# Compression tiles alternated with projection tiles, a start in halves, and the gated output moved ahead of two remainders

## The chip, the cores and the metric

One NeuronCore of a Trainium2 chip runs the whole program; seven stay idle. The metric is the device time of one execution in microseconds (us), the median of several runs. The profile is of one further execution. TensorE does matmuls, VectorE is called DVE, ScalarE ACT, GpSimd POOL and SyncE SP.

## What is computed

Two transformer blocks over 256 tokens of width 2048, all in fp32. The change touches the first block only, and of it these parts:

```python
def compress(kraw, pe, w1, w2):
    kb = kraw[:, idx] + pe[None, None, :, None, :]
    hdn = jax.nn.silu(jnp.einsum("bnlhd,ldf->bnhf", kb, w1))
    return jnp.einsum("bnhf,fe->bnhe", hdn, w2)

h = rmsnorm(x, norm_w[layer])
proj = h @ w_in[layer]
(u_pool, g_pool, q, kc_raw, vc_raw, k_sel, v_sel, k_win, v_win,
 g_nsa, g_br) = jnp.split(proj, split_at, axis=-1)
kc = rope(compress(heads(kc_raw, N_KV_HEADS), ...), cmp_pos)
vc = compress(heads(vc_raw, N_KV_HEADS), ...)
o_nsa = nsa_attention(qh, kc, vc, ksh, ..., kwh, ..., gates)
y_b = (o_nsa * jax.nn.silu(g_nsa)) @ w_nsa_out[layer]
```

`nsa_attention` has three branches (compressed keys, selected keys, window) over 16 query heads in 4 groups. Beside the blocks a modulation is computed, `mod = silu(c) @ w_ada + b_ada`, which the second block needs; its weights are multiplied on DVE.

## The kernel before

**Weight tiles.** All weights that TensorE multiplies lie in one array `ws` of 128 x 1024 tiles (512 KB), in the order of use. SP loads them into a ring of four (`raw`). ACT writes the high part `w_hi` of each (`split`, line 619), DVE the remainder `w_lo` (`split`, line 1065), and TensorE multiplies `w_hi` with `a_hi`, `w_lo` with `a_hi` and `w_hi` with `a_lo` (`tile`, lines 1805 to 1807): 12 matmuls of 512 columns for a projection tile. Semaphores bind the ring: a load waits for `lo_done` of the tile four before, ACT for the load and for `tile_used` of the tile four before, DVE for `hi_done`, TensorE for `lo_done`. `steps` on ACT and DVE writes the splits of the next tiles; what stands between two calls of it is done between two tiles. `PHASES` gives the order of the tiles, `CHUNKS` the numbers of the PSUM pairs (two pairs in turn; a pair is free when it has been evicted, semaphore `acc_free`).

**The start.** The activations are read as `x0` in four chunks. TensorE transposes them in eight turns (`x_turn`, line 1844 in the trace), ACT scales them into `a_hi` (line 832) and DVE makes `a_lo` (line 1273). Turn j + 2 stands behind tile j. The identity and the norm weights `n1T` come by POOL's queue (line 456); TensorE, ACT and DVE wait for both (`first_in`).

**Compression.** After the projections `kc`, `vc`, `ks`, `kw`, `vs`, the eight tiles `cmp_k` multiply the blocks of the compressed keys (`kb_hi`, `kb_lo`, 60 rows): 12 matmuls of 256 columns each. `vw` follows, then the eight of `cmp_v`, then the tile `gbr` (branch gates) and `q` in four chunks. The blocks are built on DVE (`block_sum`, `block_lo`) and ACT (`kb_hi`), in one buffer for both, so those of the values follow the use of the first.

**Attention.** A loop over the four groups. In each, three chunks of weight tiles (24) fill the places between four units of attention. `a.fill` gives the tiles at each place. Unit j's probabilities are transposed and multiplied in step j + 1; after it come the gated output `ot` (DVE, line 1246), `y_hi` (ACT, line 806) and `y_lo` (DVE, line 1250). The third step and the last lie at j = 3 and j = 4. Chunks 1 and 2 are merge gates: DVE adds `bias_c` to the PSUM halves into `gst` (lines 1135 and 1138), which frees each half for the next chunk (`half_free`, `half2_free`); the next group's first tile waits for them. Six halves of modulation weights (`ada`, ring of three) are multiplied and summed on DVE in each group (`modulation`, line 1079).

**POOL's queue** issues in order, in each turn of its loop (`nsa_loads`): six loads of `ada`, each waiting until the modulation that read its slot of the ring is done, then twice a load of the next `bias_c` (256 KB, line 502), each after a `gate_sum`:

```python
for k in range(loads):
    load_ada(at_i(ADA0["nsa"] + ADA_RING + k))
for c in range(2):
    pool.wait_ge(gate_sum, 2 * i + c + 1)
    pool.dma_start(bias_c[:], ...).then_inc(bias_c_in, 16)
```

The sixth `load_ada` waits for `ada_used` of this group's sixth modulation. The last group has only three loads ahead of its two of `bias_c`.

## Time and profile before

| | |
|---|---|
| median of 3 runs | 2280.42 us (2279.46 to 2280.89) |
| profiled execution | 2282.75 us, span 2281.1 us |
| TensorE (PE) busy | 2250.8 us, 99% |
| DVE busy | 1556.1 us, 68% |
| ACT busy | 1105.4 us, 48% |
| bytes moved | 546.49 MB, mean 240 GB/s |
| chain that ended last | PE 87%, DVE 6%, ACT 3%, issue 2%, DMA 2% |

The span runs from the first to the last instruction; the time of the execution has 1.65 us more around it. Matmuls overlap in the records: a 512-column one lasts 0.39 us and the next starts 0.23 us after it, so a wait shows in full only where it is longer than that overlap. In a timeline the bracket gives the engine's idle time ahead of a row and what ended it.

### The profile page before, as it was taken

The page shows a single profiled execution, that of the slowest core. Times are in us where ns is not written, and L with a number is a line of the kernel's source. Part 1 is how long each engine was busy: PE and PEld are TensorE (multiplying, and loading weights), DVE is VectorE, ACT ScalarE, POOL GpSimd, SP SyncE. Part 2 cuts the span into 40 slices and gives each one's busy share as a digit, 9 for nine tenths or more (in the row PEclk, how much of TensorE's full clock was granted, in tenths as well). Part 3 has the DMA queues.
Part 4 walks back from the last instruction along what each step waited for, and adds up shares of the span by engine and source line. Part 5 has one row for each costly group of instructions (what it writes and reads, how often), then busy time and mean ns, then how long its engine had stood idle before and what let it go on. Part 6 is the DMA issues. An engine that isn't in the chain of part 4 may idle for free.

```text
span 2281.1 us, 31278 instructions
## 1 busy us (share of the span) xinstructions
PE 2250.8 (99%) x10377; PEld 1863.9 (82%) x10377; DVE 1556.1 (68%) x1936; ACT 1105.4 (48%) x1437; POOL 149.9 (7%) x285
## 2 busy tenths in 40 slices
PE   8999999999999999999999999999999999999998
PEld 6888888788788888888888888888888888888886
DVE  5685777777776556788777776666555666655566
ACT  6454445566564444533366554445444443444444
POOL 1000110000000000011011210000000000000000
PEclk9999999999999999999999999999999999999999
DMA  8887897555665766598588886666666666666564
GB/s 286 288 283 266 302 337 253 205 193 202 211 225 175 272 209 228 199 320 292 195 284 288 311 317 248 235 217 213 210 212 221 230 222 228 227 213 208 207 205 146
DMA packets 150104, 546.49 MB, mean 240 GB/s; under 512 B 17249, under 2 KB 17392, under 8 KB 148496
## 3 DMA queue, kind: packets, MB, share of 16 engines
q1 hardware_dynamic: 112400, 406.37, 51.4%
q0 software_dynamic: 34752, 129.71, 16.3%
q10 hardware_dynamic: 2880, 9.44, 1.0%
q8 instruction: 46, 0.75, 0.1%
q14 instruction: 26, 0.21, 0.0%
HBM read 534.92 MB, written 10.53 MB: 239 GB/s over the span
## 4 chain that ended last, share of the span: by engine, by line
PE 87%; DVE 6%; ACT 3%; issue 2%; DMA 2%; DVEq 0%; ACTq 0%; SPq 0%
PE ps L1805 22%; PE ps L1807 22%; PE ps L1806 22%; PE ps L1922 5%; PE ps L1924 5%; PE ps L1923 5%; DVE w_lo L1065 2%; PE ps L1844 2%; DMA raw<-ws_dram 2%; ACT prob L787 1%; ACT w_hi L619 1%; PE ps L1981 1%; PE ps L2028 1%; DVE prob L1226 1%; PE ps L1822 0%
## 5 line engine op out<-in xcount | busy, mean ns | idle before, releaser
L1065 DVE TENSOR_TENSOR w_lo<-raw,w_hi 128x1024 fp32r<-128x1024 f32 x761 | 927.8, 1224 | 617.5 <-ACT w_hi L619 599.7
L619 ACT ACTIVATE w_hi<-raw 128x1024 fp32r<-128x1024 f32 x753 | 795.7, 1061 | 996.5 <-PE ps L1807 859.8
L1805 PE MATMUL ps<-w_hi,a_hi 128*128 128x512 f32 x1632 | 638.6, 391 | 3.4 <-DVE w_lo L1065 1.7
L1807 PE MATMUL ps<-w_hi,a_lo 128*128 128x512 f32 x1632 | 636.2, 390 | 0.0
L1806 PE MATMUL ps<-w_lo,a_hi 128*128 128x512 f32 x1632 | 636.0, 390 | 0.0
L1805 PEld LDWEIGHTS ps<-w_hi,a_hi 128*128 128x128 f32 x1632 | 306.9, 188 | 67.1 <-issue 2.2
L1807 PEld LDWEIGHTS ps<-w_hi,a_lo 128*128 128x128 f32 x1632 | 306.9, 188 | 64.1
L1806 PEld LDWEIGHTS ps<-w_lo,a_hi 128*128 128x128 f32 x1632 | 307.1, 188 | 63.1
L1922 PE MATMUL ps<-w_hi,a_hi 128*128 128x512 f32 x640 | 258.5, 404 | 0.4 <-DVE w_lo L1065 0.4
L1924 PE MATMUL ps<-w_hi,a_lo 128*128 128x512 f32 x640 | 249.8, 390 | 0.0
L1923 PE MATMUL ps<-w_lo,a_hi 128*128 128x512 f32 x640 | 249.3, 390 | 0.0
L1924 PEld LDWEIGHTS ps<-w_hi,a_lo 128*128 128x128 f32 x640 | 120.1, 188 | 25.9
L1922 PEld LDWEIGHTS ps<-w_hi,a_hi 128*128 128x128 f32 x640 | 120.3, 188 | 24.8 <-issue 1.1
L1923 PEld LDWEIGHTS ps<-w_lo,a_hi 128*128 128x128 f32 x640 | 120.4, 188 | 24.3 <-issue 1.0
L1079 DVE CUSTOM_DVE_ANT_0 ada<-ada,cb 128x1024 f32<-128x1024 f32 x108 | 131.8, 1220 | 6.4 <-DVE nms L1200 3.7
L1805 PE MATMUL ps<-w_hi,f_hi 128*128 128x512 f32 x336 | 130.8, 389 | 0.0
L1807 PE MATMUL ps<-w_hi,f_lo 128*128 128x512 f32 x336 | 130.7, 389 | 0.0
L1806 PE MATMUL ps<-w_lo,f_hi 128*128 128x512 f32 x336 | 130.7, 389 | 0.0
L1086 DVE CUSTOM_DVE_ANT_0 ada<-ada,cb 128x1024 f32<-128x1024 f32 x84 | 102.5, 1221 | 25.1 <-DMA ada<-wa_dram 24.3
L472 POOL DMA_DIRECT2D ada<-wa_dram x105 | 55.7, 531 | 715.5 <-DVE mod_part L1079 643.6
L1807 PEld LDWEIGHTS ps<-w_hi,f_lo 128*128 128x128 f32 x336 | 63.1, 188 | 13.2
L1806 PEld LDWEIGHTS ps<-w_lo,f_hi 128*128 128x128 f32 x336 | 63.1, 188 | 13.1
(310 smaller groups left out, 2125.4 us busy)
## 6 DMA issues: line engine op xcount, KB each, us to landing
raw<-ws_dram SPq DMA_DIRECT2D x769, 512.0 KB, 4.2
ada<-wa_dram POOLq DMA_DIRECT2D x192, 512.0 KB, 4.8
gates_spill<-gst ACTq DMA_DIRECT2D x16, 512.0 KB, 5.4
ga<-gates_spill POOLq DMA_DIRECT2D x8, 512.0 KB, 4.2
gb<-gates_spill POOLq DMA_DIRECT2D x8, 512.0 KB, 6.0
bias_c<-b_merge_dram POOLq DMA_DIRECT2D x9, 256.0 KB, 4.9
x<-x_dram SPq DMA_DIRECT2D x4, 512.0 KB, 7.6
cb<-c_dram POOLq DMA_DIRECT2D x2, 1024.0 KB, 5.1
```

What stands on the lines that cost most here:

```text
L472: pool.dma_start(ada[:, k.slot(ADA_RING), :], wa[k.n]).then_inc(ada_landed[k.slot(ADA_RING)], 16)
L619: act.activation(w_hi[:, k.slot(RING), :], raw[:, k.slot(RING), :], ACT.Copy).then_inc(hi_done, 1)
L1065: dve.tensor_tensor(w_lo[:, k.slot(RING), :], raw[:, k.slot(RING), :], w_hi[:, k.slot(RING), :].bitcast(F32), ALU.subtract).then_inc(lo_do ...
L1079: dve.tensor_tensor_reduce(out=a, in0=a, in1=cb[:, half * TW:(half + 1) * TW], scale=1.0, scalar=0.0, op0=ALU.mult, op1=ALU.add, accum_out ...
L1086: dve.tensor_tensor_reduce(out=a, in0=a, in1=c[:, half * TW:(half + 1) * TW], scale=1.0, scalar=0.0, op0=ALU.mult, op1=ALU.add, accum_out= ...
L1805: pe.matmul(o, hi(m, tb), w_hi[:, s, cols], start=m == 0, stop=False)
L1806: pe.matmul(o, hi(m, tb), w_lo[:, s, cols], start=False, stop=False)
L1807: mm = pe.matmul(o, lo(m, tb), w_hi[:, s, cols], start=False, stop=m == of * kts - 1)
L1844: ins = pe.transpose(ps[0:m, bank, n * P:n * P + b.shape[0]], b, ident[0:b.shape[0], 0:b.shape[0]])
L1922: pe.matmul(o, hi, w_hi[:, s, cols], start=m == 0, stop=False)
L1923: pe.matmul(o, hi, w_lo[:, s, cols], start=False, stop=False)
L1924: mm = pe.matmul(o, lo, w_hi[:, s, cols], start=False, stop=m == KT - 1)
```

## The change

1. **Start.** `ident` and `n1T` become one tensor `first`, loaded first on SP's queue. The first chunk of `x` comes in two halves on ACT's queue, the first weight tile in two halves on SP's; after them SP's order is raw 1, x 1, raw 2, x 2, raw 3, x 3. ACT loads its table with a small copy ahead of the data. TensorE multiplies zeros (`idle_turns`): 11 products of 128 columns, then the first turn, then 7 more. The first tile is split and multiplied in halves, with the second turn between them.
2. **Compression.** `BESIDE` is the order of 16 tiles: two `cmp` tiles, then by turns a projection tile and a `cmp` tile, and two projection tiles at the end. `cmp_k` goes with `vw`, `cmp_v` with `q1`; `gbr` and `q0` come between the two. The loads of `ws` are laid out in that order. `kb_hi` and `kb_lo` of the values, the transposes of the hidden rows and the first modulations of `qup` move along.
3. **Attention.** In step j = 3, `ot` is computed ahead of the two remainders and no longer behind them, and the sixth modulation moves from ahead of them to behind `y_lo`.

```diff
+BESIDE = [(1, 0), (1, 1)] + [t for j in range(6) for t in ((0, j), (1, j + 2))] + [(0, 6), (0, 7)]
 PHASES = [
-    ("kcvc", 2 * T_K), ("ks", T_K), ("kw", T_K), ("vs", T_K), ("cmp_k", 8), ("vw", T_K), ("cmp_v", 8), ("gbr", 1),
-    ("q01", 2 * T_K), ("qup", 6 * T_K), ("nsa", 4 * 3 * T_K),
+    ("kcvc", 2 * T_K), ("ks", T_K), ("kw", T_K), ("vs", T_K), ("cmp_k_vw", 2 * T_K), ("gbr", 1),
+    ("q0", T_K), ("cmp_v_q1", 2 * T_K), ("qup", 6 * T_K), ("nsa", 4 * 3 * T_K),
...
-            for k in range(RING):
+            sp.dma_start(first[:], t["first"]).then_inc(first_in, 16)
+            sp.dma_start(raw[:, 0, 0:NC], ws[0][:, 0:NC]).then_inc(raw0_in, 16)
+            sp.dma_start(raw[:, 0, NC:TW], ws[0][:, NC:TW]).then_inc(raw_landed[0], 16)
+            for k in range(1, RING):
+                sp.dma_start(raw[:, k, :], ws[k]).then_inc(raw_landed[k], 16)
                 sp.dma_start(x0[:, k], x_chunks[k]).then_inc(x_in[k], 16)
-                sp.dma_start(raw[:, k, :], ws[k]).then_inc(raw_landed[k], 16)
...
+            act.dma_start(x0[:, 0, :, 0:S], x_first[:, :, 0:S]).then_inc(x0_in, 16)
+            act.dma_start(x0[:, 0, :, S:NC], x_first[:, :, S:NC]).then_inc(x_in[0], 16)
+            act.wait_ge(t_free, 2)
+            act.activation(warm[:], cmx[:], ACT.Copy)
...
             project("vs", 4)
             hidden(0)
+            evict(5, At(G0["vw"]), ACT.Copy)
             act.wait_ge(kb_sum, 2)
-            act.wait_ge(tile_used, T0["cmp_k"] + 8)
+            act.wait_ge(tile_used, T0["cmp_k_vw"] + 2 * T_K)
             act.activation(kb_hi[:], kbf[:], ACT.Copy).then_inc(kb_hi_done, 1)
...
-                        if nsa_ and j % 2:
-                            m = 3 * (j // 2) + 2
-                            modulation(ada0 + m, m)
+                        if nsa_ and j == 1:
+                            modulation(ada0 + 2, 2)
...
                     if nsa_:
+                        if j == nu - 1:
+                            gated(u0 + (j - 1), *a.units[j - 1])
                         fill(a.fill[2 + j])
...
+                            if j != nu - 1:
+                                gated(u, tb, h0)
+                            o = ot[:].rearrange("p (h s) -> p h s", h=2)
                         dve.wait_ge(a.y_hi_done, (u + 1 + 1).n)
                         dve.tensor_tensor(lo, o, hi.bitcast(F32), ALU.subtract).then_inc(a.y_done, 1)
+                    if nsa_ and j == nu - 1:
+                        modulation(ada0 + 5, 5)
...
+            pe.wait_ge(zeros_in, 1)
+
+            def idle_turns(n):
+                for _ in range(n):
+                    pe.matmul(ps[:, 7, 0:P], squares[:, 1, 0:P], squares[:, 1, 0:P], start=True, stop=True)
+
+            idle_turns(11)
+            pe.wait_ge(first_in, 16)
...
             x_turn(0)
-            x_turn(1)
-            for j in range(T_K):
+            idle_turns(7)
+            pe.wait_ge(t_free, TG["norm1"] + 3)
+            for q in range(2):
+                if q:
+                    pe.wait_ge(lo_done, 1)
+                else:
+                    pe.wait_ge(half0_lo, 1)
...
+                if q == 0:
+                    x_turn(1)
+            mm.then_inc(tile_used, 1)
+            x_turn(2)
+            for j in range(1, T_K):
...
+                for k, (of_kb, j) in enumerate(BESIDE):
+                    if of_kb:
+                        tile(At(T0[phase] + k), pair(At(g)), j, 8, lambda m, tb: kb_hi[:, m, :],
+                             lambda m, tb: kb_lo[:, m, :], kts=4, rows=CMP_ROWS, blocks=1, width=CMP_H)
+                    else:
+                        if j == 0:
+                            pe.wait_ge(acc_free, g + 2)
+                        tile(At(T0[phase] + k), pair(At(g + 1)), j, T_K, ah, al)
```

**How it moves the instructions.** TensorE from the program's first matmul on, before (x8 means eight in a row):

```order
L1844 MATMUL ps<-ident,x_137 128x128 x8
L1805 MATMUL ps<-w_hi,a_hi 128x512
L1806 MATMUL ps<-w_lo,a_hi 128x512
L1807 MATMUL ps<-w_hi,a_lo 128x512
```

and now (`squares` holds the zeros, `first` the identity):

```order
L2074 MATMUL ps<-squares 128x128 x11
L1878 MATMUL ps<-first,x_136 128x128 x4
L2074 MATMUL ps<-squares 128x128 x7
L2100 MATMUL ps<-w_hi,a_hi 128x512
L2101 MATMUL ps<-w_lo,a_hi 128x512
L2102 MATMUL ps<-w_hi,a_lo 128x512
L2100 MATMUL ps<-w_hi,a_hi 128x512
L2101 MATMUL ps<-w_lo,a_hi 128x512
L2102 MATMUL ps<-w_hi,a_lo 128x512
L1878 MATMUL ps<-first,x_136 128x128 x4
```

The eight transposes of `x` have become four and four, with products of zeros ahead of the first four and behind them, and the second four stand in the middle of the first tile.

DVE in compression, from the first `block_sum` of the values on, before:

```order
L1299 TENSOR_TENSOR kbf<-ckT,peT 128x15x16 x4
L1065 TENSOR_TENSOR w_lo<-raw,w_hi 128x1024 x4
L1299 TENSOR_TENSOR kbf<-ckT,peT 128x15x16 x4
L1065 TENSOR_TENSOR w_lo<-raw,w_hi 128x1024 x6
L1307 TENSOR_TENSOR kb_lo<-kbf,kb_hi 128x1920
L1065 TENSOR_TENSOR w_lo<-raw,w_hi 128x1024
```

and now:

```order
L1332 TENSOR_TENSOR kbf<-ckT,peT 128x15x16 x4
L1081 TENSOR_TENSOR w_lo<-raw,w_hi 128x1024 x6
L1332 TENSOR_TENSOR kbf<-ckT,peT 128x15x16 x4
L1081 TENSOR_TENSOR w_lo<-raw,w_hi 128x1024
L1095 ISA ada,mod_part<-ada,cb 128x1024
```

with this at the end of the phase and after it:

```order
L1081 TENSOR_TENSOR w_lo<-raw,w_hi 128x1024 x3
L1108 COPY mod_66<-mod_part 128x6
L1081 TENSOR_TENSOR w_lo<-raw,w_hi 128x1024 x3
L1340 TENSOR_TENSOR kb_lo<-kbf,kb_hi 128x1920
L1081 TENSOR_TENSOR w_lo<-raw,w_hi 128x1024
```

The second `block_sum` (`kbf`) stands two splits later, and `kb_lo` has moved from behind six more splits to behind the whole phase, `gbr` and two tiles of `q0`; three of the modulations (`ada`) now lie between the splits of the phase.

DVE at the end of a group, from the probabilities of the last unit to the merge gate of the last chunk, before:

```order
L1226 TENSOR_TENSOR prob<-prob,coef 128x1024
L1079 ISA ada,mod_part<-ada,cb 128x1024
L1079 ISA mod_part 128x1
L1065 TENSOR_TENSOR w_lo<-raw,w_hi 128x1024
L1065 TENSOR_TENSOR w_lo<-raw,w_hi 128x1024
L1246 TENSOR_TENSOR ot<-ps,gT 128x256
L1250 TENSOR_TENSOR y_lo<-ot,y_hi 128x2x128
L1065 TENSOR_TENSOR w_lo<-raw,w_hi 128x1024
L1065 TENSOR_TENSOR w_lo<-raw,w_hi 128x1024
L1135 SCALAR_TENSOR_TENSOR gst_160<-ps,rstd,bias_c 128x512
L1138 SCALAR_TENSOR_TENSOR gst_160<-ps,rstd,bias_c 128x512
```

and now:

```order
L1242 TENSOR_TENSOR prob<-prob,coef 128x1024
L1250 TENSOR_TENSOR ot<-ps,gT 128x256
L1081 TENSOR_TENSOR w_lo<-raw,w_hi 128x1024
L1081 TENSOR_TENSOR w_lo<-raw,w_hi 128x1024
L1272 TENSOR_TENSOR y_lo<-ot,y_hi 128x2x128
L1095 ISA ada,mod_part<-ada,cb 128x1024
L1095 ISA mod_part 128x1
L1081 TENSOR_TENSOR w_lo<-raw,w_hi 128x1024
L1081 TENSOR_TENSOR w_lo<-raw,w_hi 128x1024
L1151 SCALAR_TENSOR_TENSOR gst_159<-ps,rstd,bias_c 128x512
L1154 SCALAR_TENSOR_TENSOR gst_159<-ps,rstd,bias_c 128x512
```

`ot` moved up past the modulation and two remainders; the modulation's two rows moved down past these remainders and `y_lo`. POOL's loop, whose last `ada` load waits for that modulation, ends as before:

```order
L475 DMA ada<-wa_dram 128x1024
L475 ISA
L475 DMA ada<-wa_dram 128x1024
L504 ISA
L505 ISA
L505 DMA bias_c<-b_merge_dram 128x512
L504 REGISTER_ALU
L505 ISA
```

These rows are the last loads of the turn and then those of `bias_c`; nothing in their order has changed.

## Rows read from the trace of the kernel before

**Rows 1.** Page, part 1; part 5: line engine op, tiles xcount | busy, mean ns | idle

```profile
PE 2250.8 (99%) x10377; PEld 1863.9 (82%) x10377; DVE 1556.1 (68%) x1936; ACT 1105.4 (48%) x1437; POOL 149.9 (7%) x285
...
L1065 DVE TENSOR_TENSOR w_lo<-raw,w_hi 128x1024 fp32r<-128x1024 f32 x761 | 927.8, 1224 | 617.5 <-ACT w_hi L619 599.7
L619 ACT ACTIVATE w_hi<-raw 128x1024 fp32r<-128x1024 f32 x753 | 795.7, 1061 | 996.5 <-PE ps L1807 859.8
```

**Rows 2.** What TensorE waited for, whole span: total us, times, longest us

```profile
PE ps L1844 <- ACT pcT L640: 4.8, 4, 1.2
PE ps L1805 <- DVE w_lo L1065: 3.2, 3, 1.7
```

**Rows 3.** Timeline of the start: start us, us, engine, line, op [idle before <-releaser]

```profile
8.05 1.97 PE L1844 MATMUL ps<-ident,x 128*128 128x128 f32 x8 [8.05 <-DMA n1T<-n1T_dram]
9.42 0.82 ACT L832 ACTIVATE a_hi<-ps,n1T 128x256 fp32r<-128x256 f32 x2
10.76 0.87 DVE L1273 SCALAR_TENSOR_TENSOR a_lo<-ps,n1T,a_hi 128x256 fp32r<-128x256 f32 x2
11.69 0.80 PE L1805 MATMUL ps<-w_hi,a_hi 128*128 128x512 f32 x1 [1.67 <-DVE a_lo L1273]
...
16.97 0.62 PE L1844 MATMUL ps<-ident,x 128*128 128x128 f32 x4
17.35 0.48 PE L1805 MATMUL ps<-w_hi,a_hi 128*128 128x512 f32 x1
...
20.19 0.60 PE L1844 MATMUL ps<-ident,x 128*128 128x128 f32 x4
```

**Rows 4.** Loads of x at the start (to landing), and fp32 matmuls in a timeline

```profile
DMA to landing us min/median/max: 4.9/7.6/9.6
...
1288.90 1.95 PE L2022 MATMUL ps<-pt,proj 128*128 128x128 f32 x16
```

**Rows 5.** Timeline of the compression tiles, TensorE, and an eviction by ScalarE

```profile
127.72 0.28 PE L1805 MATMUL ps<-w_hi,kb_hi 128*60 128x256 f32 x1
127.84 0.28 PE L1806 MATMUL ps<-w_lo,kb_hi 128*60 128x256 f32 x1
...
130.41 0.68 ACT L845 ACTIVATE proj<-ps,rstd 128x512 f32<-128x512 f32 x1
...
141.97 0.47 PE L1805 MATMUL ps<-w_hi,a_hi 128*128 128x512 f32 x1 [1.73 <-DVE w_lo L1065]
...
175.00 0.33 PE L1805 MATMUL ps<-w_hi,kb_hi 128*60 128x256 f32 x1 [0.77 <-DVE w_lo L1065]
```

**Rows 6.** Last unit of group 0: DVE, GpSimd, bias loads (439.20; another alone), TensorE

```profile
436.63 1.23 DVE L1079 CUSTOM_DVE_ANT_0 ada<-ada,cb 128x1024 f32<-128x1024 f32 x1 [0.19 <-DVE prob L1226]
437.78 2.36 DVE L1065 TENSOR_TENSOR w_lo<-raw,w_hi 128x1024 fp32r<-128x1024 f32 x2
440.06 0.42 DVE L1246 TENSOR_TENSOR ot<-ps,gT 128x256 f32<-128x256 f32 x1
...
438.52 0.53 POOL L472 DMA_DIRECT2D ada<-wa_dram  x1 [4.28 <-DVE mod_part L1079]
439.20 0.54 POOL L502 DMA_DIRECT2D bias_c<-b_merge_dram  x1
...
bias_c<-b_merge_dram POOLq DMA_DIRECT2D x1, 256.0 KB, 5.2
...
bias_c<-b_merge_dram POOLq DMA_DIRECT2D x1, 256.0 KB, 4.1
...
444.85 0.75 DVE L1135 SCALAR_TENSOR_TENSOR gst<-ps,rstd,bias_c 128x512 f32<-128x512 f32 x1
...
447.53 0.58 PE L1922 MATMUL ps<-w_hi,a_hi 128*128 128x512 f32 x1
...
459.93 1.23 DVE L1065 TENSOR_TENSOR w_lo<-raw,w_hi 128x1024 fp32r<-128x1024 f32 x1 [0.84 <-ACT w_hi L619]
```

**Rows 7.** A weight load issued between 122 and 123 us: us to landing

```profile
raw<-ws_dram SPq DMA_DIRECT2D x1, 512.0 KB, 8.2
```

More of the change, by code:

```diff
@@ L178, in const @@
             return r
-        ident = const("ident", [P, P])
+        first = const("first", [P, P + KT])
+        ident, n1T = first[:, 0:P], first[:, P:P + KT]
         trig1 = const("trig1", [P, 2, TB, HALF])
@@ L187, in build @@
         cvalid = const("cvalid", [P, TB, N_CMP])
-        n1T = const("n1T", [P, KT])
         n1T_2 = const("n1T_2", [P, KT])
@@ L454, in _ @@
         def _(pool):
-            for dst, name in ((ident, "ident"), (n1T, "n1T")):
-                pool.dma_start(dst[:], t[name]).then_inc(first_in, 16)
             for c in range(4):
@@ L857, in hidden @@
                 act.sem_inc(hdn_ready, 1)
+                steps(k + (2 * T_K - 2), 2)
             def hidden_turned(n):
@@ L892, in _ @@
                 act.activation(gates[:, tb], ps[:, 7, tb * 3 * NQ:(tb + 1) * 3 * NQ], ACT.Sigmoid, scale=rstd[:, tb:tb + 1])
-            project("q01", 7, 1)
+            hidden(1)
+            evict(7, At(G0["q1"]), ACT.Copy)
+            project("qup", 8, 0)
+            hidden_turned(1)
+            project("qup", 9, 1)
             act.wait_ge(cmp_done, 2)
             act.activation(vc[:], ps[0:N_CMP, 5, :], ACT.Copy).then_inc(cmp_ready, 1)
-            with act.Fori(0, 2) as i:
-                for c in range(2):
-                    steps(At(T0["qup"] + c * T_K, 2 * T_K, i), T_K)
-                    evict(2 * i + (8 + c), At(G0["qup"] + c, 2, i), ACT.Copy)
+            for c in range(2, 4):
+                project("qup", 8 + c, c)
             for c in range(2):
@@ L1264, in _ @@
             link(dve.memset(vcg[:], 0.0))
+            dve.memset(squares[:, 1, 0:P], 0.0).then_inc(zeros_in, 1)
             dve.memset(nmax[:, :], 0.0).then_inc(acc_free, 3)
             dve.memset(cmx[:, :], 0.0).then_inc(t_free, 2)
-            dve.wait_ge(first_in, 32)
+            dve.wait_ge(first_in, 16)
             for r in range(8):
-                split(At(r))
+                if r:
+                    split(At(r))
                 dve.wait_ge(t_hi, TH["norm1"] + r + 1)
@@ L1276, in _ @@
                 lo.then_inc(t_free, 1)
+                if r == 0:
+                    dve.wait_ge(half0_hi, 1)
+                    dve.tensor_tensor(w_lo[:, 0, 0:NC], raw[:, 0, 0:NC], w_hi[:, 0, 0:NC].bitcast(F32), ALU.subtract)\
+                        .then_inc(half0_lo, 1)
+                    dve.wait_ge(hi_done, 1)
+                    dve.tensor_tensor(w_lo[:, 0, NC:TW], raw[:, 0, NC:TW], w_hi[:, 0, NC:TW].bitcast(F32), ALU.subtract)\
+                        .then_inc(lo_done, 1)
             split(At(8))
@@ L1340, in _ @@
             dve.sem_inc(kc_roped, 1)
-            with dve.Fori(0, 3) as i:
-                n = ADA_TURN["qup"][0]
+            with dve.Fori(1, 3) as i:
                 a = At(ADA0["qup"], n, i)
@@ L2046, in _ @@
             x_turn(0)
-            x_turn(1)
-            for j in range(T_K):
+            idle_turns(7)
[5 more added lines that the diff above has]
+                    pe.wait_ge(half0_lo, 1)
+                cols = slice(q * NC, (q + 1) * NC)
+                for tb in range(TB):
+                    out = pair(g)[:, tb, :]
+                    pe.matmul(out, ah(q, tb), w_hi[:, 0, cols], start=q == 0, stop=False)
+                    pe.matmul(out, ah(q, tb), w_lo[:, 0, cols], start=False, stop=False)
+                    mm = pe.matmul(out, al(q, tb), w_hi[:, 0, cols], start=False, stop=False)
+                if q == 0:
[3 more added lines that the diff above has]
+            for j in range(1, T_K):
                 pe.wait_ge(t_free, TG["norm1"] + j + 3)
@@ L2055, in project, with hidden_beside @@
                 gemm(At(T0[name] + n * T_K), At(G0[name] + n), ah, al, T_K)
[L2057 to L2058 removed]
+            def hidden_beside(phase, n, g):
                 pe.wait_ge(kb_ready, n + 1)
[L2060 to L2061 removed]
+                pe.wait_ge(acc_free, g + 1)
+                for k, (of_kb, j) in enumerate(BESIDE):
[6 more added lines that the diff above has]
+                        tile(At(T0[phase] + k), pair(At(g + 1)), j, T_K, ah, al)
             def turn_hidden(n):
@@ L2111, in _ @@
                 mm.then_inc(cmp_done, 1)
-            with pe.Fori(0, 3) as i:
+            with pe.Fori(1, 3) as i:
                 for c in range(2):
@@ L2398, in layout @@
         "x": v["x"][0], "ws": ws, "wa": wa, "rpb": bias.transpose(0, 2, 1, 3).reshape(8, GRID_W, -1),
-        "n1T": columns(v["norm_w"][0]), "n1T_2": columns(v["norm1_w_2"][0]), "n2T_2": columns(v["norm2_w_2"][0]),
+        "first": np.concatenate([np.eye(P, dtype=np.float32), columns(v["norm_w"][0])], axis=1), "n1T_2": columns(v["norm1_w_2"][0]), "n2T_2": columns(v["norm2_w_2"][0]),
         "peT": np.stack([v["cmp_pe_k"][0].T, v["cmp_pe_v"][0].T], axis=1),
```

94 lines of the change are left out of this document (51 added, 43 removed).

## The prediction

> **What bounds the kernel now.** I read the busy shares of the page first: TensorE is busy in 99% of the span [rows 1]. So only three things can pay: stretches in which TensorE waits, matmuls at the lower clock, and fewer matmuls. The change removes no matmul, so the list of what TensorE waited for is the second view, and its sum is the ceiling: 8.0 us before the first instruction [rows 3], 4.8 us in four waits for `pcT`, 3.2 us in three waits for `w_lo` [rows 2]. The rest of the list (norms, windowed attention) is not touched. Third come the timelines of the three places [rows 3, 5, 6], to see what follows each wait. I count 0.2% of 2280 us, 4.6 us, as what a measurement can tell from no change.
>
> **Part 1, the start.** Before, TensorE's first turn of `x` runs at 8.05, released by the small load of `n1T` on GpSimd's queue, and the first tile starts at 11.69 [rows 3]. That tile takes 16.97 − 11.69 = 5.28 us for 12 matmuls, 0.44 us each for 512 columns: this is the 1.2 GHz level. The next tile takes 20.19 − 17.35 = 2.84 us, 0.24 us each: the 2.4 GHz level. It came after TensorE had worked from 11.69 on without a pause.
> The change (a) brings `ident` and `n1T` as one load, first on SyncE's queue; (b) loads the first chunk of `x` and the first weight tile in halves, x on ScalarE's queue; (c) splits the tile in halves behind the activations; (d) lets TensorE multiply zeros from about 1.9 us (DVE's second memset) on: 11 products, then 7 more behind the first turn.
> The earliest landing of a 512 KB load of `x` was 4.9 us after its issue [rows 4]. Half of it, sharing the 16 engines with the weight half, I put at 4.5 to 5 us after an issue at 1.5, so at 6.0 to 6.5. The 11 products: sixteen fp32 records of 128 columns take 1.95 us at the upper level with their tail, 0.11 us each, two to a product [rows 4]; at the lower level a product is 0.43 us and the 11 last 4.7, to 6.6. I take 6.6 for the first turn. From turn to tile, before: 11.69 − 8.05 = 3.64 us, with 8 turns, a whole split of 1.06 us on ScalarE and one of 1.23 us on DVE in between [rows 1, 3]. Now: four turns (about 0.8), `a_hi` 0.8, `a_lo` 0.9, the half `w_lo` 0.65 behind it on DVE, and hand-overs of 0.2: 3.35 us. The first tile so starts near 9.95. Its first half takes 1.37 us, the second turn 0.35, and then the second tile waits for the second `a_lo`: ScalarE `a_hi` 0.8, DVE 0.9, hand-overs, so until about 13.75, against 17.35 before. **Gain 3.6 us.** Ends: 1.1 if the clock is still low for the tile (2.5 less), 4.3 if x lands at 5.8 and the wait before the second tile shrinks. Later tiles need about 2.75 us of ScalarE each against 3.1 of TensorE and run as before. The constants on GpSimd's queue still wait for all of x, and are used 30 us later; they cost nothing.
>
> **Part 2, the compression tiles.** The eight `kb` tiles of the keys run from 127.72 to 141.97, 14.25 us for 96 matmuls of 0.117 us (11.25): 3.0 us lost; those of the values lose 1.0 in one gap that ends at 175.00 [rows 5]. Cause: a tile is used up in 1.4 us, while a ring of four wants a load, ScalarE's 1.06 and DVE's 1.23 us, and DVE has `block_sum` to do besides. Alternated with projection tiles of 2.73 us, two tiles have 4.1 us, and the ring has slack. What is late next: the pair that `vw` needs is freed by the eviction of `vs`, whose second half starts at 130.41 and takes 0.68, so 131.1 [rows 5]; two `kb` tiles end at 130.5, so TensorE waits 0.6 us there. Beside the values the eviction isn't held up by a late load, and I count 0.1. Switching between the shapes 13 more times costs at most 0.02 each: 0.2. **Gain 4.0 − 0.6 − 0.1 − 0.2 = 3.1 us**, ends 2.0 and 3.9. The sums of the modulation that move are as many as before, one to three tiles apart as elsewhere, and cost nothing; `kb_lo` of the values now lies 22 us ahead of its use.
>
> **Part 3, the last units of the four groups.** Before, DVE does the sum of the modulation (436.63), two remainders (437.78) and only then `ot` (440.06); ScalarE's `y_hi` and then its copy of `pcT` stand behind it, and TensorE's transposes wait for `pcT` [rows 2, 6]. Now `ot` comes first, at 436.6, `pcT` at about 438.7, and TensorE arrives at 440.9: the wait, 1.2 us and 0.15 of restart in each group, goes. That is 5.4 us if nothing else moves.
> But the modulation sum moves too, behind `y_lo`: it starts 0.34 (`ot`, 0.42 less its overlap) + 2.28 (two remainders) + 0.34 (`y_lo`) = 2.96 us later. GpSimd's queue runs in order: the last `ada` load of the turn waits for that sum (438.52, released by DVE) and **the load of `bias_c` stands behind it** (439.20, landing 5.2 us later, 444.4) [rows 6]. DVE reads `bias_c` at 444.85, so it had 0.45 us of slack. Now it lands at 447.4, while everything else is ready at 443.4. The first `gst` ends at 448.15, it frees the half of PSUM that the next group's first tile writes, and TensorE, there at 446.1, waits 2.1 us and starts 0.7 us later than the 447.53 of before. Behind it DVE is 2.0 us late for the next group's ropes; the wait of 0.84 (0.97 of pace) before 459.93 takes up half, and TensorE's turn of `qr`, which follows these ropes, comes **1.1 us later than before**. This holds for the three groups of the loop. The last group loads only three `ada` tiles, its bias long landed; it keeps its 1.35. **Part 3: 3 × 1.1 − 1.35 = 1.9 us lost.** Ends for a turn: from 1.35 gained (bias in time) to 4.0 lost (landing 8.2 us, as a weight load had among `ada` loads [rows 7]); I take the landing of 5.2, of this same load behind the same neighbour.
> The Trainium skill (DMA: Bandwidth & Descriptors, Anatomy of one DMA) fits a load as 2.0 us plus its bytes over 436 GB/s. By that estimate 256 KB land after 2.6 us, the bias would come before TensorE needs the half, and the sum would be 2268.3; the trace has no such landing for this load (4.1 at best).
>
> **Sum.** 3.6 + 3.1 − 1.9 = 4.8 us. The profiled execution took 2282.75 us (span 2281.1), so 2277.9 for one like it; the median of the runs lies 2.3 us under it, so **2275.6 us**.
>
> **Rivals.** *The bias load is hidden after all.* With a landing of 4.1 us, as when it was issued alone [rows 6], the groups stand 0.1 us better than before instead of 1.1 worse: 3.6 + 3.1 + 1.35 + 0.3 = 8.4 us, 2272.0; fully hidden 12.1 us, 2268.3. For it: less stands before it than one would fear. Against: the same `ada` load is ahead of it. 0.20.
> *The first tile stays slow.* If x lands late, TensorE idles behind its zeros and the clock is low for the tile; the start then brings 1.0 and the sum 2.2 us: 2278.2. The Trainium skill (TensorE: Matmul & The Clock Gate, Part 1) calls the look at activity free-running, so that the number of slow matmuls varies between runs; the trace has a single start and can't show it. 0.13.
> *The bias load turns the change over.* Its place is the same in the queue, but the weight loads of the two remainders, now issued just ahead, stand in its way. From 2.7 us a turn on, a landing of 6.9, three turns eat all gains (3.6 + 3.1 + 1.35 = 8.05); at 8.2 they cost 11.9, and the kernel is 3.9 us slower: 2284.3. For it: such landings exist [rows 7]. Against: the neighbours are as many as in the 5.2 of before. 0.07.
>
> **How the numbers follow.** The forecast as summed has 0.60, and its own range is 2273.5 to 2278. The range from 2270.5 to 2279.5 adds the slow start and the landings down to 4 us; outside lie the fully hidden load and the lost case. Faster by over 0.2% (under 2275.8): half of the forecast and the hidden load, 0.32 + 0.19 = 0.51. Slower by over 0.2%: 0.04, from the worst end of the last rival. No difference to be told: 0.45.
>
> **What would show it.** First matmul of a tile near 10 us with 0.23 us of pace, second tile near 13.7; no wait over 0.7 us among the `kb` tiles; no wait for `pcT`; instead three waits of about 2 us of TensorE for `gst` at the start of groups 2 to 4, some 87 us apart, with the bias load issued 3 us later in the turn, and none at the end of the last group. I am wrong if these three waits are absent, or if the second tile starts after 15.5.

## The result, and the profile after

The changed kernel takes **2291.63 us** (median of 5 runs, 2287.83 to 2292.09), the kernel before 2280.89 in the same comparison (5 runs, 2279.46 to 2281.54). The ratio is 1.0044, with a 95% interval of 1.003 to 1.0057. I forecast 2275.6 us, 4.8 us gained; it is **10.7 us slower**.

| | before | after |
|---|---|---|
| median | 2280.89 us | 2291.63 us |
| profiled execution | 2282.75 us, span 2281.1 | 2287.83 us, span 2286.2 |
| waits of TensorE for `pcT` | 4, 4.8 us | none |
| waits for `w_lo` among the compression tiles | 3, 3.2 us | none |
| waits for `gst` | none | 3, 12.4 us |

The profiled execution of before lies 1.9 us above its median, that of after 3.8 us below its own: the two traces show 5.1 us of the 10.7. The page of after, part 1, as in [rows 1]:

```profile
PE 2257.8 (99%) x10413; PEld 1870.2 (82%) x10413; DVE 1553.7 (68%) x1938; ACT 1104.6 (48%) x1439; POOL 148.2 (6%) x283
```

TensorE is busy for 7.0 us more. The 36 records more are the 18 products of zeros, two to a product, and they alone last 5.07 + 1.76 = 6.8 us (below, in the start); so the busy share tells nothing of the loss, and the list of waits has to. What TensorE waited for, whole span of after (total us, times, longest), against [rows 2], the two longest items:

```profile
PE ps L1956 <- DVE gst L1151: 12.4, 3, 4.8
PE ps L1878 <- DVE xn L1486: 2.6, 2, 1.4
```

The two items that the change was to remove are gone, and one line stands in their place: three waits for `gst`. Where they lie, and what DVE and GpSimd do there (timeline of after, end of the first group; columns as in [rows 3]; against [rows 6]):

```profile
430.10 0.42 DVE L1250 TENSOR_TENSOR ot<-ps,gT 128x256 f32<-128x256 f32 x1
430.44 2.35 DVE L1081 TENSOR_TENSOR w_lo<-raw,w_hi 128x1024 fp32r<-128x1024 f32 x2
432.71 0.42 DVE L1272 TENSOR_TENSOR y_lo<-ot,y_hi 128x256 f32 x1
433.05 1.22 DVE L1095 CUSTOM_DVE_ANT_0 ada<-ada,cb 128x1024 f32<-128x1024 f32 x1
...
434.92 0.53 POOL L475 DMA_DIRECT2D ada<-wa_dram  x1 [7.17 <-DVE mod_part L1095]
435.60 0.54 POOL L505 DMA_DIRECT2D bias_c<-b_merge_dram  x1 [0.15 <-issue]
...
443.76 0.75 DVE L1151 SCALAR_TENSOR_TENSOR gst<-ps,rstd,bias_c 128x512 f32<-128x512 f32 x1 [6.78 <-DMA bias_c<-b_merge_dram]
...
438.09 1.89 PE L2062 MATMUL ps<-pt,vg 128*128 128x256 f32 x8
444.57 0.80 PE L1956 MATMUL ps<-w_hi,a_hi 128*128 128x512 f32 x1 [4.58 <-DVE gst L1151]
```

Read it from the top. `ot` is early (430.10), both remainders follow (430.44), `y_lo` (432.71), and only then the sixth modulation (433.05). GpSimd waits for it and issues the last `ada` load at 434.92 and the bias load at 435.60. DVE has nothing more to do from 437 on and sits idle for 6.78 us until that load has landed; TensorE ends its last unit (438.09 and 1.89 long) and waits 4.58 us for `gst`. Then seven matmuls start 0.43 us apart. The loads issued in that stretch (KB, us from issue to landing): the `ada` load at 434.9, a weight load and the bias load at 435.6, and a weight load at 437.2:

```profile
ada<-wa_dram POOLq DMA_DIRECT2D x1, 512.0 KB, 7.6
...
raw<-ws_dram SPq DMA_DIRECT2D x1, 512.0 KB, 7.2
bias_c<-b_merge_dram POOLq DMA_DIRECT2D x1, 256.0 KB, 8.1
...
raw<-ws_dram SPq DMA_DIRECT2D x1, 512.0 KB, 7.3
```

The bias load needed **8.1 us**, against 5.2 in [rows 6]; in the two groups after it 8.3 and 6.6.

To see what each part gave, I compare one mark in both traces, the start of TensorE's turn of `qr` in each group. The first two, before:

```profile
377.57 1.09 PE L1844 MATMUL ps<-ident,qr 128*128 128x128 f32 x8
...
464.26 1.09 PE L1844 MATMUL ps<-ident,qr 128*128 128x128 f32 x8
```

And after:

```profile
371.12 1.09 PE L1878 MATMUL ps<-first,qr 128*128 128x128 f32 x8
...
462.71 1.09 PE L1878 MATMUL ps<-first,qr 128*128 128x128 f32 x8
```

At the first mark the changed kernel is 6.45 us ahead, at the second 1.55. The third lies at 550.87 before and 554.59 after, 3.72 behind, the fourth at 637.51 and 643.73, 6.22 behind. Between two marks, a group took 86.61 to 86.69 us before and 91.59, 91.88 and 89.14 after. A second mark, the last unit's matmuls `pt,vg` of each group, shows the removed wait for `pcT`: 445.99 before and 438.09 after in the first group, so 7.90 ahead, 1.46 more than at `qr`; 1.37 to 1.39 in each later group, 5.6 in all. So the three group starts cost 7.90 − 1.55 = 6.35, then 6.65 and 3.90 us. The whole: −3.0 (start) − 3.45 (compression) − 5.6 (`pcT`) + 16.9 (group starts) = +4.85, of the 5.1 between the spans.

### The profile page after: what moved, and what is told of

Same layout as the page of the kernel before. It is cut to its first block, busy times and chain, and to the rows that moved or that the text cites. A ratio compares the mean times of both kernels' runs of the same rounds, so it can differ in the third digit from the quotient of the medians.

```text
span 2286.2 us, 31290 instructions
## 1 busy us (share of the span) xinstructions
PE 2257.8 (99%) x10413; PEld 1870.2 (82%) x10413; DVE 1553.7 (68%) x1938; ACT 1104.6 (48%) x1439; POOL 148.2 (6%) x283
## 4 chain that ended last, share of the span: by engine, by line
PE 86%; DVE 6%; DMA 3%; ACT 2%; issue 2%; POOL 0%; DVEq 0%; ACTq 0%; POOLq 0%; SPq 0%
PE ps L1839 23%; PE ps L1841 23%; PE ps L1840 23%; PE ps L1956 4%; PE ps L1958 4%; PE ps L1957 4%; PE ps L1878 2%; DVE w_lo L1081 2%; DMA ada<-wa_dram 2%; DMA bias_c<-b_merge_dram 1%; ACT prob L790 1%; DMA raw<-ws_dram 1%; PE ps L2062 1%; DVE prob L1242 1%; PE ps L1854 0%
## 5 line engine op out<-in xcount | busy, mean ns | idle before, releaser
L1956 PE MATMUL ps<-w_hi,a_hi 128*128 128x512 f32 x640 | 259.7, 406 | 13.2 <-DVE gst L1151 12.4
L1839 PEld LDWEIGHTS ps<-w_hi,f_hi 128*128 128x128 f32 x336 | 63.1, 188 | 13.1
```

What stands on the lines that cost most here:

```text
L1839: pe.matmul(o, hi(m, tb), w_hi[:, s, cols], start=m == 0, stop=False)
L1956: pe.matmul(o, hi, w_hi[:, s, cols], start=m == 0, stop=False)
```

## The experiments

All times are medians; each batch had its own runs of the kernel before beside it (medians 2280.8, 2281.6 and 2281.9 us, single runs from 2278 to 2291). Ratios are to those, with their 95% intervals.

### 1. Is it the bias load's place in GpSimd's queue?

`e1_bias_first` is the changed kernel with the load of the next bias ahead of the last `ada` load of the turn:

```diff
+                def bias(c):
+                    pool.wait_ge(gate_sum, 2 * i + c + 1)
+                    pool.dma_start(bias_c[:], ...).then_inc(bias_c_in, 16)
                 for k in range(loads):
+                    if k == loads - 1:
+                        bias(0)
                     load_ada(at_i(ADA0["nsa"] + ADA_RING + k))
-                for c in range(2):
-                    pool.wait_ge(gate_sum, 2 * i + c + 1)
-                    pool.dma_start(bias_c[:], ...).then_inc(bias_c_in, 16)
+                bias(1)
```

> The changed kernel with one thing moved: GpSimd issues the load of the next bias ahead of the last ada load of each turn, so that it no longer stands behind the sixth modulation. Theory (the bias load's place in GpSimd's queue makes the three waits): no wait for gst at the starts of groups 2 to 4, no slow matmuls behind them, no wait for pcT; before less 3.0 (start), 3.45 (compression), 5.5 (pcT): 2269 us, and the runs agree within 2 us. Rival (so many loads at that moment are the cause, whatever their order): the last ada load or a weight load is late in its place, waits of 2 us and more stay, over 2277 us.

Measured: **2271.41 us** (2269.80 to 2272.74), ratio 0.9957 (0.9943 to 0.9971). Of its waits the longest item, at the norms, and the only one for `gst`; then GpSimd's timeline at the end of the first group:

```profile
PE ps L1882 <- DVE xn L1490: 2.5, 2, 1.7
...
PE ps L1960 <- ACT gst L720: 1.0, 1, 1.0
```

```profile
426.77 0.53 POOL L475 DMA_DIRECT2D ada<-wa_dram  x1 [13.55 <-DVE mod_part L1099]
427.45 0.54 POOL L503 DMA_DIRECT2D bias_c<-b_merge_dram  x1
434.48 0.53 POOL L475 DMA_DIRECT2D ada<-wa_dram  x1 [6.49 <-DVE mod_part L1099]
```

TensorE waits for no `gst` of DVE any more (the 1.0 us for one of ACT's lies in the second block), no slow matmuls stand in the groups, and a group takes 85.2 us from one turn of `qr` to the next, 1.4 less than before. The bias load is issued at 427.45 and lands in 3.6 us; DVE reads it at 436.42. The last `ada` load still goes out among the weight loads, at 434.48, and takes 7.0 us; nothing waits for it. So the rival falls: the `ada` load is slow in that stretch also behind the bias load, but only the bias load had somebody waiting. The median is 2.4 us above the theory's 2269, and the runs agree within 2.9 us, not 2. This version beats both kernels.

`e2_mod_ahead` changes DVE's order instead and leaves GpSimd's alone:

```diff
                     if nsa_:
                         if j == nu - 1:
                             gated(u0 + (j - 1), *a.units[j - 1])
+                            modulation(ada0 + 5, 5)
                         fill(a.fill[2 + j])
...
-                    if nsa_ and j == nu - 1:
-                        modulation(ada0 + 5, 5)
```

> The changed kernel with the sixth modulation back ahead of the two remainders, right behind the gated output (which stays early). Theory: the bias load is issued some 0.4 us later than in the kernel before and lands in 5 to 5.5 us; waits for gst of 0.3 us at most a turn, pcT gone: 2269 to 2271 us. Rival (the early gated output, not the modulation, upsets the loads): waits for gst of 2 us or more stay, over 2278 us.

Measured: 2274.28 us (2270.73 to 2276.27, 7 runs), ratio 0.9964 (0.9951 to 0.9978). Its profile has one wait for a `gst` of DVE's, 0.2 us, and none for `pcT`; its bias load at the end of the first group is issued at 432.57 and landed after 6.3 us (6.1 and 6.3 in the next two groups), where 5 to 5.5 were expected. The rival falls: the early `ot` alone makes no long wait. The median is 3 us above the theory's band, that of its profiled execution (2271.9) at its edge. In that profile stand three waits of 1.8 us in all, 0.7 the longest, of TensorE for DVE's ropes ahead of turns of `qr` (line 1175), which the theory had not counted.

### 2. The parts apart

`e3_part3_undone` takes the third part back; `e4_part3_alone` is the kernel before with it and nothing else. The edit is the third group of hunks of the diff above, taken back:

```diff
-                        if nsa_ and j == 1:
-                            modulation(ada0 + 2, 2)
+                        if nsa_ and j % 2:
+                            m = 3 * (j // 2) + 2
+                            modulation(ada0 + m, m)
...
                     if nsa_:
-                        if j == nu - 1:
-                            gated(u0 + (j - 1), *a.units[j - 1])
                         fill(a.fill[2 + j])
...
-                            if j != nu - 1:
-                                gated(u, tb, h0)
+                            gated(u, tb, h0)
...
-                    if nsa_ and j == nu - 1:
-                        modulation(ada0 + 5, 5)
```

or, in `e4_part3_alone`, put into the kernel before with these signs turned round.

> The changed kernel with its third part taken back whole (start and compression alone). Theory: before less 3.0 and 3.45 us, 2274.4 us, four pcT waits of 1.2 us as before. Rival (start or compression cost something later that the checkpoints of the traces miss): over 2277 us.

Measured: 2276.46 us (2273.41 to 2278.92, 11 runs), ratio 0.9983 (0.9974 to 0.9992), four `pcT` waits, 4.6 us in all. That is between the two numbers given. The interval of the ratio is 1.8 to 5.9 us gained and leaves out the 6.4 of the theory, though in its own trace the first turn of `qr` is 6.95 us ahead of before, and the fourth 6.94. Where the other runs lose some 2 us is open: the profiled execution (2273.41 us) is the fastest of the 11.

> The kernel before with the third part alone. Theory: three waits for gst with landings of the bias load of 6.5 us or more: 11.5 us (from the profiled execution) to 17 us (from the medians) slower than before, 2292 to 2298 us. Rival (it takes the earlier arrival of TensorE from parts 1 and 2 to make the waits, or their loads' phase): under 2287 us.

Measured: 2294.62 us (2289.53 to 2297.65), ratio 1.0056 (1.0042 to 1.007). Waits of its profile:

```profile
PE ps L1930 <- DVE gst L1135: 13.7, 3, 5.1
```

The loss does not need parts 1 and 2. The third part alone costs 13.8 us, and its removal from the changed kernel saves 15.2: the same within what such medians tell. The bias loads landed in 8.6, 7.8 and 7.8 us.

`e6_start_alone` and `e7_compression_alone` are the kernel before with the hunks of the first and of the second part of the diff above (SP's, ACT's, DVE's and TensorE's starts; `BESIDE`, the phases and what goes with them), for instance:

```diff
+            idle_turns(11)
+            pe.wait_ge(first_in, 16)
...
-            hidden(0)
-            project("vw")
+            hidden_beside("cmp_k_vw", 0, G0["cmp_k"])
```

the two lines ahead of the "..." in `e6_start_alone`, the exchange behind it in `e7_compression_alone`.

> The kernel before with the new start alone. Theory, from the two traces: second tile at 14.3 instead of 17.35 us, first tile at the upper clock, 3.0 us gained, 2277.8 us. Rival (the start's gain is used up before compression, where the weight ring is empty anyway): within 1 us of before.

> The kernel before with the new order of the compression tiles alone. Theory: the three waits for w_lo (3.7 us of pace) go and nothing takes their place, 3.4 us gained, 2277.4 us. Rival (the alternation brings back a wait for the evicted PSUM pair, or the moved modulations delay something in front of the groups): less than 2 us gained.

Measured: 2277.14 us (ratio 0.9984, 0.9974 to 0.9993) and 2277.33 us (0.9975, 0.9964 to 0.9986). Both parts gain, and both rivals fall. By the ratios the gains are 3.7 and 5.7 us, with intervals some 4 to 5 us wide, so their size is better read from the traces: in those of the two runs the first turn of `qr` is 3.4 and 3.1 us ahead of before, 6.5 together, and in that of the changed kernel the two gains are 3.0 and 3.45. (The profiled execution of `e7_compression_alone`, 2282.17 us, is the slowest of its 11 runs; up to `qr` it has lost nothing.)

### 3. Why the load takes 8 us

The bias load was late for two reasons, and they can be told apart: it is issued later, and it is slower. `e5_bias_late_alone` keeps the late release but issues the bias load ahead of the `ada` load; `e9_no_ada_beside` puts that `ada` load behind the second bias load as well.

```diff
                 for k in range(loads):
+                    if k == n - 1:
+                        pool.wait_ge(ada_used, (at_i(ADA0["nsa"] + ADA_RING + k) + (1 - ADA_RING)).n)
+                        bias(0)
                     load_ada(at_i(ADA0["nsa"] + ADA_RING + k))
-                for c in range(2):
...
+                if loads < n:
+                    bias(0)
+                bias(1)
```

```diff
-                for k in range(loads):
+                for k in range(min(loads, n - 1)):
                     load_ada(at_i(ADA0["nsa"] + ADA_RING + k))
+                if loads == n:
+                    pool.wait_ge(ada_used, (at_i(ADA0["nsa"] + ADA_RING + n - 1) + (1 - ADA_RING)).n)
+                bias(0)
+                bias(1)
+                if loads == n:
+                    load_ada(at_i(ADA0["nsa"] + ADA_RING + n - 1))
```

(`bias` as in `e1_bias_first`; the first diff is `e5_bias_late_alone`, the second `e9_no_ada_beside`.)

> The changed kernel with the bias load still released by the sixth modulation, but issued ahead of the ada load that waits for the same, not behind it. It tells a late issue from a slow transfer. If only the late issue and the ada load ahead matter: landing in 4 to 5 us after an issue 0.7 us earlier, waits of TensorE for gst of 1 to 1.5 us at three starts with the clock kept up, about 2274 to 2276 us. If the burst (two weight loads ahead, two beside it) is what makes it slow: a landing of 6.5 us or more, waits of 3 us and slow matmuls behind them, 2281 us or more.

Measured: 2284.30 us (2280.72 to 2287.66, 11 runs), ratio 1.0012 (1.0003 to 1.0021); landings of 6.3, 7.3 and 7.3 us.

> The changed kernel with the bias load still released by the sixth modulation, and the ada load that waits for the same issued later, behind the second bias load. It leaves the bias load beside weight loads alone. If the ada load beside it is what makes the transfer slow: a landing of 4 to 5 us, waits of TensorE of 1 us, no slow matmuls, 2274 to 2276 us. If the weight loads of the remainders, which the change brings forward against it, are enough: a landing of 6 us or more and waits of 2 us and more, 2280 us or more.

Measured: 2279.61 us (2276.90 to 2286.14; one run of 13111 us lies outside all others), ratio 0.9993 (0.9982 to 1.0003); landings of 5.9, 6.0 and 6.7 us. The wait for `gst`, and the load at the end of the first group, of `e5_bias_late_alone` and of `e9_no_ada_beside`:

```profile
PE ps L1963 <- DVE gst L1158: 8.6, 3, 3.2
...
bias_c<-b_merge_dram POOLq DMA_DIRECT2D x1, 256.0 KB, 6.3
```

```profile
PE ps L1963 <- DVE gst L1158: 6.2, 3, 2.6
...
bias_c<-b_merge_dram POOLq DMA_DIRECT2D x1, 256.0 KB, 5.9
```

The first is the second outcome of its expectation, but for one landing of 6.3 us, one wait of 2.3 and, behind another of 3.2, no slow matmuls. For the second run both outcomes had been drawn too sharply: its landings are near those of the weight-load case, its waits of 1.8, 1.9 and 2.6 us and its time a little under it. With the same late release, the landings are 8.1, 8.3, 6.6 us behind the `ada` load, 6.3, 7.3, 7.3 ahead of it, and 5.9, 6.0, 6.7 without it; in the kernel before they were 5.2, 5.3 and 5.3. So beside weight loads alone it already takes 0.7 to 1.4 us more than before, and the `ada` load ahead adds up to 2.3. In times, by the ratios to the kernel before: from `e1_bias_first` to `e9_no_ada_beside`, that is for the late release beside weight loads alone, some 8 us; from there to `e5_bias_late_alone`, for the `ada` load behind it, some 4 more; and from there to the changed kernel, for the `ada` load ahead of it, some 7 more. Each of these steps is uncertain by 3 to 4 us.

What the changed kernel has beside the bias load shows in the list of issues: a weight load of 433.0 (in flight until 437.2), the `ada` load, the weight load of 435.6, that of 437.2. Before, the two remainders came behind the modulation, so their weight loads went out at 439.2 and 440.3, beside and behind the bias load, and no weight load in the 10 us ahead of it. Then the DMA engines, from the bias load's issue to its landing (us, busy time and instructions of PE, PEld, DVE, ACT, POOL, granted clock, DMA share, GB/s). Changed kernel, and kernel before:

```profile
435.60:441.40 5.80, 4.38 (x20) 3.39 (x18) 1.23 (x1) 1.67 (x3) 0.54 (x1) 1.00 0.82 304
441.40:443.70 2.30, 0.00 (x0) 0.00 (x0) 0.00 (x0) 0.00 (x0) 0.00 (x0) 1.00 0.28 112
```

```profile
439.20:442.20 3.00, 1.85 (x9) 1.20 (x7) 1.90 (x4) 1.59 (x4) 0.54 (x1) 1.00 0.83 287
442.20:444.40 2.20, 2.10 (x11) 1.81 (x12) 1.72 (x2) 1.97 (x4) 0.00 (x0) 1.00 0.98 309
```

In the first 5.8 us they move 1.76 MB at a busy share of 0.82 (0.83 in the first 3.0 us before); then the share falls to 0.28 and 2.3 us pass at 112 GB/s, while DVE and TensorE wait. The kernel before has no such tail: its share is 0.98 up to the landing. So 2.3 of the 8.1 us are not a want of bandwidth, but a burst that drains slowly at its end. The same view over the last 2 us ahead of each landing, for the three bias loads of each run:

| run | the `ada` load, and weight loads | landing, us | DMA share in the last 2 us |
|---|---|---|---|
| before | ahead; none under way longer | 5.2, 5.3, 5.3 | 0.97, 0.96, 0.89 |
| `e2_mod_ahead` | ahead; none under way longer | 6.3, 6.1, 6.3 | 0.80, 0.77, 0.86 |
| changed kernel | ahead; one under way for 2.6 us | 8.1, 8.3, 6.6 | 0.25, 0.21, 0.87 |
| `e10_changed_again` | the same | 7.9, 8.4, 7.7 | 0.63, 0.21, 0.37 |
| `e4_part3_alone` | the same | 8.6, 7.8, 7.8 | 0.37, 0.20, 0.68 |
| `e5_bias_late_alone` | behind; one under way for 2.0 us | 6.3, 7.3, 7.3 | 0.97, 0.89, 0.93 |
| `e9_no_ada_beside` | none; one under way for 2.0 us | 5.9, 6.0, 6.7 | 0.97, 0.98, 0.80 |

All eight landings of 7.7 us and more end in a tail, with a share of 0.68 or less, and none of the thirteen up to 7.3 does. Every one of these bias loads has further weight loads beside and behind it. The eight have besides both the `ada` load, 0.7 us ahead in the same queue, and a weight load already under way; with only one of the two there is no tail, with both there is one in eight cases of nine. The `ada` load ahead is slow there itself: 6.6 to 8.2 us, against 3.4 to 3.6 in the kernel before.

What the tail is made of can be read from the packets in the trace. Between 441.6 and 443.6 a packet of 4 KB still lasts 0.16 us, as most do elsewhere, and at four of five instants exactly four are in flight, never fewer, where the kernel before has 16 or more at three of four instants of its last 2 us. That fits four engines that work on without a pause, with the other twelve done, and not sixteen that all work at a quarter. In the second group it is mostly two. Which engines these are, and why so much is left for them, the trace does not say.

### 4. The clock

`e8_no_idle_turns` is `e1_bias_first` without the 18 products of zeros at the start.

```diff
-            idle_turns(11)
             pe.wait_ge(first_in, 16)
...
             x_turn(0)
-            idle_turns(7)
```

> The kernel with the bias load first (which took 2271.4 us) without the products of zeros at its start. Theory (they buy the upper clock for the first tile): the first tile at 0.43 us a matmul until some matmuls of the second, the second tile 2 us later than 14.3, 2273.4 us. Rival (the wait for the second turn's activations hides the slow matmuls): second tile within 0.5 us of 14.3, no difference in time; or, with the first turn no longer behind the zeros, up to 0.5 us faster.

Measured: 2272.83 us (2270.88 to 2275.11), ratio 0.9960 against the 0.9957 of `e1_bias_first`: no difference that the medians can tell (+1.4 us). Its start, TensorE:

```profile
10.24 0.76 PE L2102 MATMUL ps<-w_hi,a_hi 128*128 128x512 f32 x1 [2.68 <-DVE w_lo L1309]
...
14.65 0.58 PE L2104 MATMUL ps<-w_hi,a_lo 128*128 128x512 f32 x1
15.06 0.39 PE L2102 MATMUL ps<-w_hi,a_hi 128*128 128x512 f32 x1
...
16.11 0.48 PE L1843 MATMUL ps<-w_hi,a_hi 128*128 128x512 f32 x1
```

And that of `e1_bias_first`, with the products:

```profile
9.89 0.47 PE L2104 MATMUL ps<-w_hi,a_hi 128*128 128x512 f32 x1 [1.12 <-DVE w_lo L1309]
...
13.79 0.50 PE L1843 MATMUL ps<-w_hi,a_hi 128*128 128x512 f32 x1
```

Without them each of the first nine matmuls is followed by the next after 0.41 us or more, the full pace comes back at 15.06, and the second tile starts at 16.11 instead of 13.79 (14.32 in the changed kernel): 2.3 us, near the 2 us expected. The place of the theory is right, and both rivals fall by the trace; that the median shows only 1.4 us of it is within its spread.

`e10_changed_again` is the changed kernel unaltered.

> The changed kernel once more, for a second profile and for a comparison on this chip. The first profile took 2287.8 us, its four other runs 2290.5 to 2292.1. Theory: where the time is near 2291 us, the third wait for gst is as long as the first two (4.6 us or more) and has slow matmuls behind it, or more of them stand behind the first two. Rival: the rest lies elsewhere, and the three waits are as in the first profile.

Measured: 2290.68 us (2288.94 to 2293.37, 6 runs), ratio 1.0043 (1.0031 to 1.0055). The first matmul of group 2, that of group 4, and one further on:

```profile
444.05 0.79 PE L1956 MATMUL ps<-w_hi,a_hi 128*128 128x512 f32 x1 [4.37 <-DVE gst L1151]
...
626.93 0.50 PE L1956 MATMUL ps<-w_hi,a_hi 128*128 128x512 f32 x1 [4.18 <-DVE gst L1151]
...
628.06 0.63 PE L1957 MATMUL ps<-w_lo,a_hi 128*128 128x512 f32 x1
```

The waits for `gst` sum to 13.3 us, against 12.4. The third is 4.2 us here, against 3.1 in the first profile, and seven slow matmuls stand behind it (from 628.06 on), where the first had none. The profiled execution took 2289.2 us, 1.4 above the first. Its third group takes 91.3 us from `qr` to `qr`, against 89.1. The bias loads landed in 7.9, 8.4 and 7.7 us. The theory is borne out in its direction only: no run at 2292 us has a profile, so how the last 3 us divide is open. A pointer, not a proof, is the mean granted clock of each run: 0.997 for both profiled executions, 0.994 to 0.996 for the other nine of the changed kernel, 0.999 for most of before. The profile of `e4_part3_alone` has 0.994, and there 11 slow matmuls stand behind each of the three waits, 2.2 to 2.4 us a time.

## Why the prediction was wrong

**Where to look: right.** What the two traces differ by is TensorE's waits, and the slow matmuls behind some of them. The changed kernel's waits moved to the place named: three waits for `gst` at the starts of groups 2 to 4, none at the end of the last group, with the bias load issued 3 us later in the turn (435.60 − 430.10 = 5.50 us behind the start of `ot`, which stands where the modulation had stood, against 439.20 − 436.63 = 2.57: 2.93, where I had 2.96).

**Part 1, start: right, 3.0 us for 3.6.** The first turn was at 6.68 (forecast 6.6) and the tile at the upper clock, but it started at 10.41 and not 9.95, the second tile at 14.32 and not 13.75. The step that was short is from turn to tile: 3.73 us against my 3.35. After's start (columns as in [rows 3]):

```profile
1.82 5.07 PE L2074 MATMUL ps<-squares 128*128 128x128 f32 x22 [1.82 <-DVE squares L1289]
...
6.68 1.05 PE L1878 MATMUL ps<-first,x 128*128 128x128 f32 x4
...
7.54 1.76 PE L2074 MATMUL ps<-squares 128*128 128x128 f32 x14
7.83 0.84 ACT L841 ACTIVATE a_hi<-ps,first 128x256 fp32r<-128x256 f32 x2 [3.68 <-PE ps L1878]
...
8.79 0.88 DVE L1299 SCALAR_TENSOR_TENSOR a_lo<-ps,first,a_hi 128x256 fp32r<-128x256 f32 x2 [7.00 <-ACT a_hi L841]
...
9.59 0.68 DVE L1305 TENSOR_TENSOR w_lo<-raw,w_hi 128x512 fp32r<-128x512 f32 x1
...
10.41 0.47 PE L2100 MATMUL ps<-w_hi,a_hi 128*128 128x512 f32 x1 [1.12 <-DVE w_lo L1305]
...
14.32 0.50 PE L1839 MATMUL ps<-w_hi,a_hi 128*128 128x512 f32 x1
```

The four turns took 1.05 us, against 0.60 from 11.88 on: the pace of the lower clock (the profile's granted clock reads 1.00 over the whole start, so the level is read from the pace alone there). And `a_hi` began 1.15 behind the first of them, where I had 0.8.

**Part 2, compression: right, 3.45 for 3.1.** The wait of 0.6 us that I put beside `vs` did not come, nor the 0.2 for changes of shape (the matmuls go on 0.12 and 0.23 us apart across them), yet 3.45 is less than the 4.0 I started from; the other 0.5 is not traced. ACT evicts `vs` earlier against the tiles now:

```profile
126.54 0.68 ACT L860 ACTIVATE proj<-ps,rstd 128x512 f32<-128x512 f32 x1
...
127.56 0.40 PE L1839 MATMUL ps<-w_hi,a_hi 128*128 128x512 f32 x1
```

so it is done at 127.2, 0.3 us ahead of the first `vw` tile. I had taken the eviction's time from the old trace, where a weight load had held up the split ahead of it by 2.55 us.

**Part 3: the step that failed.** "I take the landing of 5.2, of this same load behind the same neighbour", from which the 1.1 us a turn follow. It was 8.1, 8.3 and 6.6 us. The release moved by 3 us against the weight loads as well, and so the load fell among others. My last rival said this and gave the price, and I gave it 0.07, since "the neighbours are as many as in the 5.2 of before". They are one more, the weight load of 433.0, and the burst that they make has a slow tail. My words had the second cause in them, the `ada` load ahead, but took it for harmless because it had been so before. That other neighbours change the landing with the release as late is shown by `e5_bias_late_alone` and `e9_no_ada_beside` (5.9 to 7.3 us); that the release itself is the cause of the loss, by `e1_bias_first`.

**A cost left out, of the rival too.** The wait itself came as its landing says: with 8.1 us instead of 5.2, the first tile of group 2 should start 0.7 + 2.9 = 3.6 us later against before, and it moved from 6.45 ahead at `qr` to 447.53 − 444.57 = 2.96 ahead, 3.5. But behind it, in the first two groups, seven and nine matmuls ran near 0.43 in place of 0.23 us, with the restart some 1.7 us each time (in the third none did). I had priced the lower clock at the start of the kernel and nowhere else, though my own forecast put waits of 2 us into a stream at 2.4 GHz. So the group starts cost 16.9 us where the forecast had 3 × 2.45 = 7.35.

**The range** ended at 2279.5, and its far rival at 2284.3. With a landing of 8.2 us known from a row of this trace, and a release that I had worked out to be 3 us late, the lost case should have had a larger share.

## What to carry to other kernels

- When an instruction moves on one engine, list what waits for it on the others and what is queued behind those waits. Here one modulation, moved past two remainders on DVE, held back a bias load on GpSimd whose buffer DVE had last read at 404.6, 31 us before the load went out. One line in GpSimd's order, with DVE's left as the change had it, turned 10.7 us lost into 9.4 gained.
- The landing time of a load belongs to its moment, not to the load. A load that is moved relative to a ring's refills takes the price of its new neighbours: look up what is in flight at the new issue time, and take the late end of what the trace shows into the forecast, not only into a rival.
- A new wait of TensorE of some 2 us or more is priced with the slow matmuls that may follow it: none, or 1.3 to 2.4 us here.
